# Twenty-four projection units placed later in the first stage, and four cache copies asked for by routed heads

## What is computed

```python
z = x @ w_in                       # q, k, v (8 heads x 64), GLU value and gate (512 channels each)
att  = dilated attention over q, k, v          # three branches, merged by their denominators
conv = silu(LN(depthwise_conv31(value * sigmoid(gate))))
x1 = LN(ALPHA * x + concat(att, conv) @ w_out)
# PEER: per token and head the best 16 of 128 x 128 expert pairs
q = x1 @ w_query;  s = q . sub_keys;  experts = top16(top16(s0) + top16(s1))
y = LN(ALPHA * x1 + sum_k gate_k * gelu(x1 . u[expert_k]) * v[expert_k])
# outputs besides y: k, v and conv state of both groups; the sample group's caches
# (8 requests x 2048 rows x 512, keys and values) moved on by 8 rows
```

## Time and profile before

| | |
|---|---|
| median of 3 runs | 3594.93 us (3591.83 to 3596.64) |
| profiled execution | 3579.77 us |
| its span | 3577.8 us |
| busy, share of the span | PE 71%, VectorE 78%, ScalarE 19%, GpSimd 35% |
| moved by DMA | 1394 MB, 390 GB/s on average |
| of that, gathers' queue | 1141 MB, 78.2% of the engines' time |
| granted TensorE clock, mean | 0.847 of full |

### The profile page before, as it was taken

The page is one execution under the profiler, slowest core; times in us unless marked ns, Lnnn a source line. Parts: engine busy times, 40 slices in busy tenths (PEclk is TensorE's granted clock), DMA queues, the critical chain, the costliest instruction groups (busy, mean ns, idle before and its releaser), DMA issues.

```text
span 3577.8 us, 39531 instructions
## 1 busy us (share of the span) xinstructions
PE 2524.6 (71%) x13744; PEld 1161.4 (32%) x13744; DVE 2792.9 (78%) x7476; ACT 681.3 (19%) x1481; POOL 1265.3 (35%) x1092
## 2 busy tenths in 40 slices
PE   7965468416766876687668767876787667689776
PEld 5434235412232223232323222333233322234321
DVE  5179656899889978996899689969996985356975
ACT  1210222003200320042014201420142002221010
POOL 0022112223443443444434433544344432233242
PEclk8987779757878988898879987988898888899899
DMA  9998997998999999999999999999999999999898
GB/s 336 365 360 299 339 341 274 412 362 338 421 420 385 390 421 421 412 392 421 421 410 397 421 421 396 412 421 421 393 421 421 421 415 421 419 418 389 325 378 336
DMA packets 219687, 1394.07 MB, mean 390 GB/s; under 512 B 28568, under 2 KB 39320, under 8 KB 67800
## 3 DMA queue, kind: packets, MB, share of 16 engines
q0 software_dynamic: 156672, 1140.92, 78.2%
q1 hardware_dynamic: 41264, 141.83, 10.7%
q10 hardware_dynamic: 21552, 108.79, 7.7%
HBM read 1378.32 MB, written 80.04 MB: 408 GB/s over the span
## 4 chain that ended last, share of the span: by engine, by line
DVE 42%; PE 23%; DMA 22%; issue 10%; ACT 1%; POOL 1%; SPq 0%; POOLq 0%; ACTq 0%; DVEq 0%
DMA t<-in_expert_uv,t 20%; DVE t L1067 13%; PE psum L1420 8%; PE psum L1270 5%; DVE t L934 4%; PE psum L1348 4%; DVE psum L1096 3%; PE psum L1377 2%; DVE t L1081 2%; DVE t L1015 2%; DVE t L1013 2%; DVE t L1016 2%; DVE t L1014 2%; DVE t L1012 1%; POOL t L627 1%
## 5 line engine op out<-in xcount | busy, mean ns | idle before, releaser
L627 POOL DMA_INDIRECT t<-in_expert_uv,t x1088 | 1265.1, 1163 | 2279.5 <-PE psum L1416 865.7
L1420 PE MATMUL psum<-t,t 64*64 64x512 f32 x4576 | 1289.2, 702 | 694.9 <-DVE t L1081 689.7
L1067 DVE CUSTOM_DVE_ANT_0 t<-t,t 128x1024 f32<-128x1024 f32 x1088 | 1320.8, 1221 | 449.8 <-DMA t<-in_expert_uv,t 434.3
L1420 PEld LDWEIGHTS psum<-t,t 64*64 64x64 f32 x4576 | 324.4, 151 | 1483.7 <-DVE t L1081 866.5
L1416 PE MATMUL psum<-t,t 64*64 64x512 f32 x2592 | 788.0, 737 | 0.0
L780 ACT ACTIVATE t<-t 128x2 f32<-128x2 f32 x544 | 110.6, 203 | 1996.6 <-DVE t L1067 1961.0
L1377 PEld LDWEIGHTS psum<-t,t 128*128 128x128 f32 x2304 | 291.9, 209 | 72.2 <-issue 57.6
L1377 PE MATMUL psum<-t,t 128*128 128x128 f32 (+1 forms) x2304 | 302.5, 295 | 8.7 <-ACT t L749 6.5
L1270 PE MATMUL psum<-t,t 128*128 128x128 f32 (+2 forms) x768 | 264.0, 505 | 7.1 <-DMA t<-in_xT 6.3
L934 DVE SCALAR_TENSOR_TENSOR t<-t,t,t 128x128 f32<-128x128 f32 x840 | 238.0, 345 | 0.0
L1416 PEld LDWEIGHTS psum<-t,t 64*64 64x64 f32 x2592 | 179.5, 154 | 0.0
(11 more groups left out here) (136 smaller groups left out, 2140.4 us busy)
## 6 DMA issues: line engine op xcount, KB each, us to landing
t<-in_wq_t ACTq DMA_DIRECT2D x72, 1024.0 KB
out<-in_cache_k_win SPq DMA_DIRECT2D x8, 4080.0 KB, 43.9
out<-in_cache_v_win SPq DMA_DIRECT2D x8, 4080.0 KB, 39.8
t<-in_w_in_t ACTq DMA_DIRECT2D x44, 512.0 KB, 7.5
t<-in_kc_t SPq DMA_DIRECT2D x8, 2560.0 KB
t<-in_vc_t SPq DMA_DIRECT2D x8, 2560.0 KB
t<-in_expert_uv,t POOLq DMA_INDIRECT x1088
t<-in_w_v_t ACTq DMA_DIRECT2D x6, 1024.0 KB
```

Of the source, the lines that this page charges most:

```text
L627: pool.indirect_dma_start(ring[:, r, :], None, I["expert_uv"], bass.IndirectOffsetOnAxis(ap=idn[t % 2][:, column(t, s):column(t, s) + 1], ...
L1067: dve.tensor_tensor_reduce(out=ring[:, r, 0:D], in0=x1[t % 2][:, :], in1=ring[:, r, 0:D], scale=1.0, scalar=0.0, op0=ALU.mult, op1=ALU.add ...
L1420: last = pe.matmul(MAIN[t][half][NS * a:NS * a + NS, :], zt[NS * a:NS * a + NS, k % Z_RING, j, :], vv[NS * a:NS * a + NS, :], start=(c == ...
```

## The change

`UNIT_GROUP` of pass 1 puts unit 0 at group 0, right behind the first head's scores, unit 1 at group 14 and the other 22 at groups 16 to 31: 16, 16, 17, 18, 18, 19, 20, 21, 21, 22, 23, 24, 24, 25, 26, 26, 27, 28, 29, 29, 30, 31. The gate products (one group later) and the stores of GLU (two groups later) follow, since `GATE_GROUP` is taken from `UNIT_GROUP`. Pass 2 stays.

Of the first eight cache copies, numbers 0 to 3 keep their waits. Numbers 4 to 7 wait until 1, 3, 5 and 7 heads of tile 0 are routed.

```diff
-UNIT_GROUP = [[10 + j * 21 // 24 for j in range(24)], [j * 2 // 3 for j in range(24)]]
+UNIT_GROUP = [[0, 14] + [16 + j * 16 // 22 for j in range(22)], [j * 2 // 3 for j in range(24)]]
...
             for i in range(PH):
-                if i:
+                if i == 0:
+                    sp.wait_ge(proj_done, UNIT_AT[1] - 2)
+                elif i < PH // 2:
                     sp.wait_ge(sm_done, i)
                 else:
-                    sp.wait_ge(proj_done, UNIT_AT[1] - 2)
+                    sp.wait_ge(a_route, 2 * i - PH + 1)
                 copy_cache(i)
             sp.dma_start(gluS[:, :, :, 0:PAST], I["state_t"]).then_inc(state_in, 16)
             sp.dma_start(st_o, I["state_conv"][0, :, NT:PAST, :]).then_inc(st_out, 16)
```

## The result

| | before | changed |
|---|---|---|
| median of 19 runs each | 3586.4 us | 3598.0 us |
| ratio | | 1.0032, 95% interval 1.0019 to 1.0046 |
| profiled execution | 3579.8 us | 3595.9 us |
| its span | 3577.8 us | 3594.0 us |
| PE's first scores of tile 1 | 389.6 us | 404.8 us |

The kernel became 0.32% slower, 11.5 us of 3586. The median of before was 3594.9 us in the three runs the prediction had and 3586.4 in nineteen; a single run of either kernel lies up to 16 us off its median, so only the ratio carries the comparison of times. The traces, one execution each, are used to compare places in the first stages.

What follows compares the result with a forecast made beforehand. The change was worth what it moves tile 1's start, set by SP's load of q: -18.7 + 8 + 22 = +11.3, with roundings +11.5 us, 3606.5 at the median; own range 3598 to 3615, 8 in 10 within 3586 to 3626.

Steps and rivals of the forecast that it cites:

- route of head 0 starts: VectorE's first route in tile 0, predicted at 147.6 us, 16.6 us earlier, after 6.9 of 23.5 go back.
- fifth dot: VectorE's fifth dot product of tile 0, predicted 18.7 us earlier, with 2 us gained in waits.
- q behind the seventh head: q for tile 1 lands 53 us behind the seventh routed head, not 30.9; tile 1's front 22 us later.
- the rest: Stages after tile 1's start move as a whole, carrying its shift unchanged to the end.
- The signs that I had named: First gather near 158 us, SP held some 35 us, unchanged later stages; wrong if landings held VectorE over 20 us.
- The units: PE's projection units of pass 1 moved to other groups: head 0's route starts 16.6 us earlier.
- The first gathers: First five dots of tile 0: spacing left some 5 us, 2 us of waits gained, 18.7 at the fifth.
- Copies 4 to 6: Cache copies beside tile 0's gathers lose 1, 5 and 2 us; seventh routed head 10.7 us earlier.
- Rival 2: Ring of five buffers starves at 5 us a gather beside a copy: +30 us, 3620 to 3632; 13%.
- SP's tail: On SP's queue, copy 7, state, xT and q pile up before tile 1: 53 us, start 22 us later.
- Rivals 1: State's pieces and xT slip in beside copy 7, q lands 35 us behind the seventh head: 3580 to 3588; 12%.
- 4: Late weights and the gate product eat the units' 23.5 us: 3620 to 3625; 5%.

Runs made afterwards that it cites:

- e1: Changed kernel with the eight cache copies back at their old waits, so only the units of pass 1 move: ratio 0.9967 to the kernel before.
- e3: Changed kernel with the convolution state's load and copy moved ahead of copies 4 to 7 on SP: ratio 1.0012 to the kernel before.
- e7: On top of e1, all 24 units of pass 1 late, one at group 17 and 23 over groups 18 to 31: ratio 0.9940.
- e10: Changed kernel with xT, the state's load and its copy put behind tile 1's loads of q, GLU and x on SP: ratio 1.0056.
- e2: Changed kernel with the units put back, so only copies 4 to 7 wait for routed heads: ratio 1.0107 to the kernel before.
- e5: On top of e3, copies 4 to 7 all asked for behind tile 1's loads of q, GLU and x: ratio 0.9915.
- e4: On top of e3, copy 7 alone asked for behind tile 1's loads of q, GLU and x: ratio 0.9992.
- e9: On top of e8, the load of xT for pass 2 put behind tile 1's loads of q, GLU and x: ratio 0.9920.
- e8: On top of e5, the late units of e7: median 3551.5 us, ratio 0.9915 to the kernel before.

## Why the prediction was right

It said 3606.5 on a median of 3594.9, 11.5 us slower; the ratio gives 11.5 us. By its steps, with the time by which tile 1's start moved:

| step | predicted | profile and runs |
|---|---|---|
| first weight transposes | 72.3 us | 72.4 in e1, 72.9 in e3; 74.3 in the changed kernel, by another path |
| route of head 0 starts | -16.6 us | -17.1 (147.07) |
| fifth dot | -18.7 | -16.0 (189.48 against 205.44) |
| seventh routed head | -10.7 | -4.5 |
| q behind the seventh head | 53 us, +22 | 50.7, +19.7 |
| tile 1 starts | +11.5 | +15.2 |
| the rest | 0 | +1.0 in the profiled spans |

The signs that I had named came: the first gather was asked for at 157.4 us, SP was held for 31.7 us, and landings held VectorE 11.8 us between the fifth dot and the seventh head, under the 20 that would have meant wrong.

**The units: right, the last half microsecond by luck.** The walk along PE's order gave the route's start to half a microsecond, and the gate product that stands before the route on VectorE is a cost that a look at the unit times alone would have missed. The other such cost, late weights and a cold clock at group 0, is what e1 shows: unit 0 waited 4.3 us, ran in 10.0 us at a mean granted clock of 0.71 (60 to 70 us; 0.50, the lower level, in the first half) and ended late. In the changed kernel's own profile it did not come about. There the last v weights of pass 0 landed later, and the first scores stood at 64.29 and not at 54.69:

```profile
64.29 0.48 PE L1292 MATMUL psum<-t,t 64*128 64x128 f32 x2 [0.47 <-ACT t L646]
64.70 7.13 PE L1272 MATMUL psum<-t,t 128*128 128x512 f32 x16
```

Unit 0 followed without a wait, in 7.1 us at a granted clock of 1.00. The projection then started at 99.79 (98.5 predicted) and the key scores ended at 132.05 (132.4). e7 and e10 have the late start too (61.99 and 60.68), the other kernels don't; why is open. e1 shows that this head start lasts: 14.0 of its 18 us reach tile 1.

**The first gathers: wrong sign.** I gained 2 us there; the first dot waited 13.3 us and not 9.4, and the head start fell from 17.1 at the route to 16.0 at the fifth dot. Copy 4 beside the first gathers is no better than the old backlog.

**Copies 4 to 6: undersized.** I took 8 us. Between the fifth dot and the seventh head the change shows 11.5, and e2 shows 12 in all; against e5, with no copy under any dot, the first ones included, it is 18.6. I had also read the waits before the change too high there: the two windows of the earlier trace rows share the 3.4 us of the fifth dot, so behind it stood 1.3 us (20.7 in all less 19.4) and not 4.8. It became 11.8, 10.5 us more. The term came from a mean pace of 4.0 us a dot; with five buffers I now take it to be the pace between two routes, 3.5 us, that meets the 4.3 to 5 us of a gather beside a copy. No run tried that apart. Rival 2 had this mechanism, at twice its size.

**SP's tail: right in mechanism and nearly in size.** Copy 7 took 27.8 us and not 34, the state 7.7 behind it and not 11.4, xT and q 14.9 and not 7.6; the sum was 2 us off. The last of these was the wrong one: I priced the state's copy and xT at 421 GB/s, the rate of all engines, after I had priced copy 7 at the 138 GB/s of SP's queue beside the gathers. At 138 the 2.2 MB come to 16 us; from the state's landing to xT's it was 14.1. And one step was misread, as e10 shows: tile 1 waits for xT as much as for q. In the changed kernel the two land within a microsecond, so it made no difference there. The 4 us that copy 7 costs the last dots were hidden, as said (e4 shows them uncovered).

**The number: closer than its terms.** Up to the seventh head the prediction was 6.2 us too early (2.7 at the fifth dot, 3.5 in the copies), and 2.3 us too long in the tail: 3.9 us at tile 1's start, +15.2 in place of +11.3. The profiled spans moved by 16.2. That the ratio gives just the forecast 11.5 is luck. That the rest moves as a whole is borne out: over the change and the ten experiments the medians moved within 7 us of the start of tile 1's front (of the first unit of pass 2 in e9 and e10), from -33.7 against -30.1 us in e8 to +35.4 against +31.1 in e2. Rivals 1 (the tail doesn't reach tile 1) and 4 (the units gain nothing) are ruled out by the change's own trace and by e1.

## What to carry to other kernels

A transfer that is asked for later takes all that stands behind it on its queue along. Before a copy is moved into idle DMA time, look which load is the next one that somebody waits for on the same queue, and what lands between. Here the same four copies cost 31 us under the gathers and in front of that load, and about 2 us right behind it. The place for them was a stage with a DMA share of 0.84 that kept its length when the share rose to 1.00, not a stage in which VectorE lives from five ring buffers. And where one load is taken out of a tail, ask which other one the first instruction behind it needs.

## What the runs showed of the hardware

- SP's queue moved at about the same rate beside the gathers with pieces of 1.8 KB and of 4 KB. xT of pass 2, 1792 KB in pieces of 1.8 KB, landed in 12.7 us in the kernel before, 12.9 in e1 and 12.8 in e5, 142 to 145 GB/s; copy 7, in pieces of 4 KB, made 150 GB/s in the changed kernel. In e9 and e10 xT took 20.1 and 22.6 us because it wasn't alone: SP's queue moved 2.77 and 3.06 MB in that time, 138 and 135 GB/s, of which xT is 1.84. With the 120-byte pieces of the state it was slower: 480 KB in the 7.7 us between the landings of copy 7 and the state, 64 GB/s. SP's queue while xT was under way, in the kernel before and in e9 (packets, MB, share of the engines):

```profile
q1 hardware_dynamic: 1040, 1.84, 42.6%
```

```profile
q1 hardware_dynamic: 1285, 2.77, 35.9%
```

- Asking for a transfer can hold the engine that asks for very long: 68.6 us in e1 for 352 KB, behind a copy and a load of 4096 rows of 120 bytes; in e3, where they stood ahead of the gathers, the copy held SP for 14.8 us. It costs only what that engine has to do next.
- A copy of 4080 KB landed in 27.8 us beside the gathers of tile 0 and held VectorE for some 4 us (e2: 12.1 us more for copies 4 to 6); four more of them beside PE's projection units made that stage 2 us longer in all (e5).
